# A paged latent-attention decode stage whose cache pages are turned by VectorE in 32 by 32 blocks

## The reference, cut to what matters

```python
c_past = cache_ckv[page_table].reshape(b_s, past_len, KV_RANK)     # 8 x 2048 x 256
kpe_past = cache_kpe[page_table].reshape(b_s, past_len, HEAD_ROPE) # 8 x 2048 x 32
s = einsum('bqhr,bkr->bhqk', q_lat, c) + einsum('bqhe,bke->bhqk', q_pe, kpe)
p = softmax(s * scale)            # 16 heads, 2048 cached positions and the new one
term = einsum('bhqk,bkr->bqhr', p, c)
```

## Time and profile before

| | us |
|---|---|
| median of 3 runs | 2010.53 |
| lowest and highest run | 2008.69, 2016.31 |
| span of the profiled execution | 2007.1 |
| head pairs end, decode loop begins | about 1507 |
| last values of the decode loop end | 1585.1 |

### The profile page before, as it was taken

The page is one execution under the profiler, slowest core; times in us unless marked ns, Lnnn a source line. Parts: engine busy times, 40 slices in busy tenths (PEclk is TensorE's granted clock), DMA queues, the critical chain, the costliest instruction groups (busy, mean ns, idle before and its releaser), DMA issues.

```text
span 2007.1 us, 41612 instructions
## 1 busy us (share of the span) xinstructions
PE 1960.4 (98%) x17604; PEld 1875.2 (93%) x17604; DVE 1277.0 (64%) x1771; ACT 820.4 (41%) x1243; POOL 132.8 (7%) x231
## 2 busy tenths in 40 slices
PE   8999999988999999999999999999989999999999
PEld 7999999987999999999999999997666799999998
DVE  6445486697469577576884856655764349668474
ACT  5332233343245244255452534454654244345252
POOL 3002002010000000000000000000047000000000
PEclk9999999989999999999999999999999999999999
DMA  7233234864342322234322322231248422323222
GB/s 151 84 102 88 75 93 115 269 140 100 95 137 85 120 89 95 77 105 116 97 85 85 127 85 86 84 101 51 54 119 231 149 71 83 127 85 120 91 74 75
DMA packets 260624, 211.55 MB, mean 105 GB/s; under 512 B 42372, under 2 KB 235426, under 8 KB 260450
## 3 DMA queue, kind: packets, MB, share of 16 engines
q1 hardware_dynamic: 248528, 187.52, 31.9%
q0 software_dynamic: 6656, 13.69, 2.4%
q10 hardware_dynamic: 5266, 7.85, 1.2%
HBM read 195.29 MB, written 10.33 MB: 102 GB/s over the span
## 4 chain that ended last, share of the span: by engine, by line
PE 67%; DVE 3%; ACT 2%; issue 2%; SPq 1%; DMA 1%; DVEq 0%; ACTq 0%
PE ps L2459 25%; PE ps L2487 25%; PE ps L2388 6%; PE ps L2401 2%; PE ps L2947 1%; PE ps L3053 1%; PE ps L3209 1%; PE ps L3086 1%; SPq L654 1%; SPq L639 1%; DMA cb<-cache_ckv 1%; PE ps L2841 1%; PE ps L3030 1%; DVE wl L1668 0%; DVE xl L1619 0%
## 5 line engine op out<-in xcount | busy, mean ns | idle before, releaser
L2388 PE MATMUL ps<-xh,wh 128*128 128x260 f32 x1088 | 286.9, 285 | 2.6 <-DVE xl L1619 1.4
L2388 PE MATMUL ps<-xl,wh 128*128 128x260 f32 x1088 | 283.7, 283 | 0.0
L2487 PE MATMUL ps<-xoh,wh 128*128 128x260 f32 x992 | 281.3, 284 | 1.3 <-DVE sq L1835 1.3
L2487 PE MATMUL ps<-xoh,wl 128*128 128x260 f32 x992 | 281.0, 283 | 0.0
L2487 PE MATMUL ps<-xol,wh 128*128 128x260 f32 x992 | 280.6, 283 | 0.0
L2459 PE MATMUL ps<-xh,wh 128*128 128x260 f32 x872 | 228.8, 284 | 0.6 <-DVE wl L1668 0.6
L1067 ACT ACTIVATE wh<-rw 128x1024 fp32r<-128x1024 f32 (+1 forms) x135 | 138.8, 1029 | 218.6 <-PE ps L2459 151.7
L2459 PE MATMUL ps<-xl,wh 128*128 128x260 f32 x872 | 227.0, 282 | 0.0
L2388 PE MATMUL ps<-xh,wl 128*128 128x260 f32 x1088 | 219.3, 283 | 0.0
L990 ACT ACTIVATE wh<-raw 128x1024 fp32r<-128x1024 f32 (+1 forms) x90 | 100.4, 1116 | 283.4 <-PE ps L2388 250.5
L2388 PEld LDWEIGHTS ps<-xh,wh 128*128 128x128 f32 x1088 | 205.6, 189 | 6.9 <-issue 3.9
(11 more groups left out here) (550 smaller groups left out, 4202.2 us busy)
## 6 DMA issues: line engine op xcount, KB each, us to landing
rw<-ffn_w_gate SPq DMA_DIRECT2D x33, 1024.0 KB, 5.4
rw<-ffn_w_up SPq DMA_DIRECT2D x33, 1024.0 KB, 8.0
rw<-ffn_w_down SPq DMA_DIRECT2D x12, 2048.0 KB, 7.8
raw<-ffn_w_gate SPq DMA_DIRECT2D x22, 512.0 KB, 3.9
raw<-ffn_w_up SPq DMA_DIRECT2D x22, 512.0 KB, 3.9
raw<-ffn_w_down SPq DMA_DIRECT2D x16, 704.0 KB, 4.8
rw<-ffn_w_down SPq DMA_DIRECT2D x6, 1536.0 KB, 6.7
cb<-cache_ckv SPq DMA_DIRECT2D x72, 128.0 KB, 3.7
```

The source lines that it names most:

```text
L2388: got = mm(ps[0:width, bank + half, 0:HALF], w[par_][:, k * width:k * width + width], src[:, k0 + k, half * HALF:half * HALF + HALF], star ...
L2487: got = mm(ps[:, bank + mat, T0], w[:, cols], src[:, j, k, :], start=first and k == 0 and m == 0 and s == 0, stop=k == 3 and m == 1, skip_ ...
```

## The change

- A page is read as 32 rows of 4 KB (four tokens each) into 32 partitions: page g goes to the partitions 32 (g mod 4) and up. The rotary key is read as 32 rows of 512 bytes. The number of DMAs and the queue of each stay.
- VectorE turns a sequence in five instructions (`V.transpose`, 32 x 32 blocks): one of 512 elements a partition for the rotary key, four of 1024 for the latent. PSUM, TensorE and ScalarE have no part in it. The 36 TensorE turnings and the 9 copies of a sequence are gone.
- A 32 x 32 block leaves 32 channels on each group of 32 partitions, so the scores become tiles of 32 rows and 32 columns, four row groups by four column groups, 128 tokens in each: 16 matmuls for the rotary key and 32 for each of four parts of the latent, 144 in all (288 records). They write four PSUM banks (0 to 3), one for each row group. There is one set of banks: `past_scores(b, 0)` waits for the exponentials of b - 1.
- The queries are needed on each row group. POOL writes `qlat` to DRAM and reads it back with eight DMAs (`dr_q`, `qrep`), once, before its pages. `qpe` loses its zero padding.
- TensorE's order in one turn is: turning of the probabilities of b, scores of b + 1, values of b. The copy to `pbT` goes from VectorE to ScalarE.
- `wo_half(0, 0, ...)` is split and goes into the last pair of heads and into the first scores. `wide_hi` and `wide_lo` move behind the last probabilities. The banks of `wo_half` and of small tiles change.

```diff
                 for g in ckv:
-                    eng.dma_start(cb[j][:, g, :], inp["cache_ckv"][bass.ds(numbers[b][g], 1)].rearrange("a p r -> p (a r)")).then_inc(arrived[j], 16)
+                    eng.dma_start(page(cb[j], g), inp["cache_ckv"][bass.ds(numbers[b][g], 1)].rearrange(
+                        "a (u v) r -> (a u) (v r)", v=ROWS)).then_inc(arrived[j], 16)
...
+            def turned(b, c):
+
+                if c == 0:
+                    dve.wait_ge(d_in[b % 3], (b // 3 + 1) * 16 * N_SP)
+                    dve.wait_ge(d_kin[b % 3], (b // 3 + 1) * 16 * N_POOL)
                 if b >= 1:
-                    dve.wait_ge(d_s, b)
+                    dve.wait_ge(d_s, (NCT + 1) * (b - 1) + c + 1)
+                if c == 0:
+                    V.transpose(kbT, kb[b % 3].rearrange("p g e -> p (g e)")).then_inc(d_t, 1)
+                else:
+                    V.transpose(cbT[:, c - 1, :, :].rearrange("p q (g u) -> p g q u", u=HP),
+                                cb[b % 3][:, :, 2 * HP * (c - 1):2 * HP * c].rearrange("p g (q r) -> p g q r", q=2)).then_inc(d_t, 1)
...
             for b in range(NB):
-                dve.wait_ge(d_s, b + 1)
-                own(V.tensor_reduce(mb[:, b:b + 1], ps[:, 2 + b % 2, :], AX.X, ALU.max))
+                if b + 1 < NB:
+                    turned(b + 1, 0)
+                    turned(b + 1, 1)
+                dve.wait_ge(d_s, (NCT + 1) * (b + 1))
+                own(V.tensor_reduce(mb[:, b:b + 1], ps[:, 0:NQ, 0:P], AX.XY, ALU.max))
                 ts(nmb[:, b:b + 1], mb[:, b:b + 1], -SCALE, None, ALU.mult).then_inc(d_m, 1)
                 if b + 1 < NB:
-                    turned(b + 1, 1)
-                    turned(b + 1, 3)
-                else:
-                    wide_lo(0)
-                dve.wait_ge(d_pt2, b + 1)
-                if b >= 1:
-                    dve.wait_ge(d_o, b)
-                copy(pbT[:, :, :], ps[:, 4, :].rearrange("p (m q) -> p m q", m=NQ)).then_inc(d_pe, 1)
-                if b + 1 < NB:
-                    turned(b + 1, 5)
-                    turned(b + 1, 7)
+                    for c in range(2, NCT + 1):
+                        turned(b + 1, c)
...
+            def past_scores(b, c):
+
+                if b == 0 and c == 0:
+                    pe.wait_ge(d_qr, 16 * (1 + 2 * NQ))
+                if b >= 1 and c == 0:
+                    pe.wait_ge(d_e, b)
+                pe.wait_ge(d_t, (NCT + 1) * b + c + 1)
+                for q in range(2 if c else 1):
+                    n = 2 * (c - 1) + q
+                    for a in range(NQ):
+                        rows = slice(HP * a, HP * a + HP)
+                        w, keys_ = (qrep[n // NQ][rows, n % NQ, b, :], cbT[rows, c - 1, q, :]) if c else (qpe[rows, b, :], kbT[rows, :])
+                        for j in range(NQ):
+                            got = mm(ps[HP * j:HP * j + HP, a, 0:P], w, keys_[:, P * j:P * j + P],
+                                     start=c == 0, stop=c == NCT and q == 1, skip_group_check=True)
+                got.then_inc(d_s, 1)
```

More of the change, by code:

```diff
@@ L1531, in _ @@
                     act.wait_ge(d_pt2, b)
[L1532 to L1537, removed]
+                run(pb.rearrange("p (v a u) -> p a v u", v=ROWS, a=NQ), ps[:, 0:NQ, 0:P].rearrange("p a (v u) -> p a v u", v=ROWS),
+                    ACT.Exp, bias=nmb[:, b:b + 1], scale=SCALE, accum_out=lb[:, b:b + 1]).then_inc(d_e, 1)
+                if b >= 1:
+                    latents(b - 1)
+                act.wait_ge(d_pt2, b + 1)
+                run(pbT[:, :, :], ps[:, 4, :].rearrange("p (m q) -> p m q", m=NQ), ACT.Copy).then_inc(d_pe, 1)
+            wide_hi(0)
             act.wait_ge(d_w, 1)
@@ L2263, in _ @@
                     maximum(i + 1, 2)
+                else:
+                    turned(0, 0)
                 probs(i, 3)
@@ L3150, in _, with wo_half @@
                     values(1, n // 2)
[L3151 to L3166, removed]
+            def wo_half(d, half, k0, k1):
+                if d == 3 and half == 1:
+                    pe.wait_ge(x_upd, UPD["wo"] + 1)
+                pe.wait_ge(w_lo, WO0 + d + 1)
+                hi_, lo_ = (wh[(WO0 + d) % 2], wl[(WO0 + d) % 2]) if d < 2 else (w4h[:, d - 2], w4l[:, d - 2])
+                for k in range(k0, k1):
+                    for m, (w, srcs_) in enumerate(((hi_, (xh, xl)), (lo_, (xh,)))):
+                        for s, src in enumerate(srcs_):
+                            got = mm(ps[:, WO_BANKS[d][half], 0:HALF], w[:, k * P:k * P + P], src[:, k, half * HALF:half * HALF + HALF],
+                                     start=k == 0 and m == 0 and s == 0, stop=k == KD - 1 and m == 1)
+                if half == 1:
+                    got.then_inc(w_used, 1)
             for i in range(NH // 2):
@@ L3186, in _ @@
                 if not more:
-                    turned(0, 0)
+                    pe.wait_ge(a_ol, NH // 2 - 2)
+                    wo_half(0, 0, 0, 3)
                 turned_probs(i, 4)
+                turned_probs(i, 5)
                 if not more:
-                    turned(0, 1)
-                turned_probs(i, 5)
+                    wo_half(0, 0, 3, NH // 2 - 2)
                 if 2 <= i < NH // 2 - 2:
                     values(i // 2 + 1, i % 2)
-            for q in range(2, 6):
-                turned(0, q)
@@ L3196, in _ @@
             weighted(NH // 2 - 1)
[L3197 to L3210, removed]
-                if half == 1:
-                    got.then_inc(w_used, 1)
@@ L3237, in _ @@
+            for c in range(3):
+                past_scores(0, c)
+            pe.wait_ge(a_ol, NH // 2)
+            wo_half(0, 0, NH // 2 - 2, KD)
+            for c in range(3, NCT + 1):
+                past_scores(0, c)
+            for b in range(NB):
                 pe.wait_ge(d_e, b + 1)
@@ L3243, in _ @@
                 if b + 1 < NB:
-                    for q in range(4, 9):
-                        turned(b + 1, q)
-                else:
-                    turn(ps[0:NB, 7, 0:P], mb[:, :])
-                    turn(ps[0:NB, 7, P:2 * P], lb[:, :]).then_inc(d_rt, 1)
-                    wo_half(1, 0, 0, 3)
+                    for c in range(NCT + 1):
+                        past_scores(b + 1, c)
+                else:
+                    turn(ps[0:NB, 0, 0:P], mb[:, :])
+                    turn(ps[0:NB, 0, P:2 * P], lb[:, :]).then_inc(d_rt, 1)
+                    wo_half(1, 0, 0, 4)
                 pe.wait_ge(d_pe, b + 1)
@@ L3465, in _ @@
                 number(b)
+            pool.wait_ge(l_qe, 1)
+            pool.dma_start(dr_q, qlat[:, :, :, :].rearrange("p r b h -> p r (b h)")).then_inc(d_qr, 16)
+            pool.wait_ge(d_qr, 16)
+            for a in range(NQ):
+                for r in range(RT):
+                    pool.dma_start(qrep[r][HP * a:HP * a + HP].rearrange("p s b h -> p s (b h)"),
+                                   dr_q.rearrange("(s p) r n -> r p s n", s=NQ)[r]).then_inc(d_qr, 16)
             caches()
```

115 lines of the change are left out of this document (45 added, 70 removed).

## The result

The changed kernel takes 2052.12 us (median of 4 runs, 2046.46 to 2055.44), the kernel before 2009.61 beside it: a ratio of 1.0206, with a 95% interval of 1.0187 to 1.0225. It is 42 us slower; 2001.9 was forecast, 50 us less. Its profiled execution took 2046.46 us with a span of 2044.7.

The account below looks back on a forecast made before the run. SyncE's page queue (9.76 us a sequence) was taken as the loop's bound, DMA engines and TensorE close behind. -10.3 + 1.7 = -8.6 us takes 2007.1 to 1998.5; plus 3.4 over the span, 2001.9 us, range 1990 to 2018.

Parts of the forecast that it names:

- Queues: SyncE's page queue: same 17 DMAs, 333 ns an issue, held-up issues go, so a period of 8.76 us.
- a sign of being wrong: Forecast is wrong if VectorE never waits in the loop, SyncE waits long for values, or an issue isn't 333 ns.
- Landing: Time from last page issue to data arrived: taken at 3.7 us with longer rows, bounds 2.5 and 5.8.
- The rival: Page loads into 32 partitions land slower, 200 GB/s instead of 292 at full share: 2017 us, chance 0.07.
- Turning on VectorE: Page transposes on VectorE: 1.22 us per 1024 elements, 5.6 us a sequence; with maximum and negative 6.7 a period.
- Scores: TensorE's 288 small score records take 2.0 to 4.3 us a sequence; only the last part, 0.45 to 0.95, on the path.
- One set of score banks: Scores of b + 1 wait for exponentials of b, about 1.9 us, covered by values of the sequence before (1.9).
- The loop that the buffers close: `pages(b + 3)` waits for values of b: 17.7 us for two periods, 8.8 each, level with the queue; 9.0 taken.
- The clock: TensorE, half idle, may fall to half clock: period taken as 9.0 us instead of 8.8, and 1.7 at the end.
- The start and the end: First maximum at 1510.9, `pages(3)` near 1518.1, `pages(7)` at 1554.1, last probabilities turned at 1571.2 against 1581.48: 10.3 us earlier.

Follow-up runs that it names:

- the last experiment: Changed kernel with old short page rows, maximum ahead of the turnings, and 256-column score tiles (144 records): 2012.01 us, ratio 1.0007 to the kernel before.

## Why the prediction was wrong

**Queues: the price right, the step beside the point.** An issue took 316 ns in the median and nine mostly 4.3 to 4.7 us, as forecast; but held-up issues did not go (up to 1.41 us for one, and 5.48 and 6.36 for nine). And SyncE no longer sets the period: both page queues wait for values, which the forecast had named as a sign of being wrong.

**Landing: taken at 3.7 us, measured 8.4, 6.7 and 5.9 behind the last three issues on the chain.** The rival had the mechanism and the rate: 200 GB/s guessed, 202 measured where the engines were full. Its price was 15 us above the forecast, at a chance of 0.07; alone in the kernel before the rows cost 7 to 9, in the changed kernel 12.5. The Trainium skill, "SBUF — State Buffer", section "Door 1: The DMA port swizzle", gives 189 GB/s for 32 partitions, measured at transfers of 1 MiB. The runs are near it and a little above, with four groups of partitions in flight; I had argued that those would lift it to 292, and they don't.

**Turning on VectorE: right.** 32 transposes of 1024 elements:

```profile
L2256 DVE STREAM_TRANSPOSE cbT<-cb x32: 1201/1203/1236, 1499.7 to 1604.9; 128x1024 f32<-128x1024 f32 x32
```

**Scores: the term that failed most. The record was right, its delivery and its clock were put at nothing.** Between gaps, at a granted clock of 1.00, the starts are 13 ns apart: the group below has 66 starts in 1.16 us less one record's 0.29.

```profile
1526.98 1.16 PE L3215 MATMUL ps<-cbT,qrep 32*32 32x128 f32 x66
```

So the floor of about 25 ns of the Trainium skill ("TensorE: Matmul & The Clock Gate", section "Wait — 56ns, not 53.3ns?") does not hold for matmuls in different tiles, as the earlier trace rows had said. At half clock they are 22 ns apart (128 in 2.80 us above). But the 288 records took 6.6 to 12.6 us a sequence and not 2.0 to 4.3: 2.0 to 5.8 of it idle time for instructions in the sequences on the chain, and the rest at half clock in large part. Neither was in the term for the scores, and instructions were in no rival. The runs put the price of the many small records at 22.2 us, the largest of all. The hint was in the size of the change: 36 turnings and 48 score records became 288 of 13 ns each, so a packet of instructions is used up in 1.7 to 2.8 us.

**One set of score banks: the step that put the scores on the path.** I wrote that the values of the sequence before cover maximum, negative and exponentials, and that only the last part of the scores is on the loop. In TensorE's order those values stand behind the scores of b + 1, and in VectorE's order two turnings of b + 1 stand ahead of the maximum of b. So the exponentials of b, all scores of b + 1 and then the values follow the landing of b + 1, one after another. By the forecast's own prices this mistake was small: two turnings 1.9, maximum to exponentials 1.9, probabilities 0.5 and all scores 2.0 to 4.3 are 6.3 to 8.6 us, where it had 7.2. It became dear by the scores. The maximum ahead of the turnings gave back 9.2 us; the values ahead of the scores gave back nothing.

**The loop that the buffers close: forecast 17.7 us, measured 32.7.** I had put five turnings, the maximum and the last part of the scores on it (7.2 us). In their place stand 15.1: two turnings 1.9, maximum to exponentials 1.6, probabilities 1.1, all scores 10.5 (4.29 of it idle). The landing added 4.7 to its 3.7, the values 3.0 to their 1.9, most of it clock. The sum of the terms was right in form (period = half of this loop) and wrong in three of its entries: the scores by 6 to 8 us, the landing by 4.7, the values by 3.0.

**The clock.** The forecast let its fall cost 0.2 us a period (9.0 for 8.8) and 1.7 us at the end. It is at half for much of the loop (0.70 in the mean of 1507 to 1600): turning and values cost 2.5 us a sequence more. What it would have cost with a period of 9 us isn't shown; with 10.4, in the last experiment, it was at full in four of the seven stretches of 10 us from 1510 to 1580 and the values took 1.86 to 1.91.

**The start and the end.** The first maximum came at 1510.20 against a forecast of 1510.9. `pages(3)` came at 1524.0 and not 1518.1, because the values of sequence 0 already stood behind the scores of 1, 7.8 us with 2.03 idle. From `pages(7)` to the mark it was 29.1 us and not 17.1, by the same terms as in the loop.

What the pieces gave, in us: short rows 12.5, maximum first 9.2, half as many records 22.2, all together 40.1 of 42.5. They overlap, since the short rows also took 12 us off the waits for instructions. How much of the rows' 12.5 is landing and how much is fetch stays open: in the two profiles the landings on the chain are 4.9 us less and the gaps inside the scores on it 7.7 us less (9.5 for 17.2), and some 5 us of that go back to longer issues and the rest of the chain. So does whether a second set of score banks would have paid: it wasn't tried, since a set takes four of the eight banks and the rest hold probabilities, outputs and `wo_half`.

## What to carry to other kernels

Before replacing a few long matmuls by many short ones, count instructions: here TensorE got 256 in some 6 to 8 us beside busy DMA engines (1.9 to 2.8 running, the rest waiting) and in 3.5 to 4.0 us beside quiet ones, whatever its tiles could do. When a change takes a second set of buffers away, write the new order of every engine down for two iterations and look for the first instruction of b + 1 that stands ahead of the last of b; a wait for a transfer in front of it puts the landing into every period. And take DMA rows together with the partitions that they reach: four times longer rows into a quarter of the partitions moved pages a third slower here.

## What the runs showed of the hardware

- TensorE's instructions come in packets of 16 KB, 256 of them, over the same DMA engines as data. In dense code of small matmuls a packet costs a gap, unless TensorE waits for something else meanwhile: 0.6 to 1.8 us with quiet engines, mostly 2.4 to 5.2 beside pages or weights.
- Page loads of 32 partitions by 4 KB ran at about 200 GB/s at full share, 128 partitions by 1 KB at 292.
- Small matmuls in sixteen tiles start 13 ns apart at a granted clock of 1.00 and 22 ns apart at 0.50; in eight tiles (half of the scores) 28 ns apart, 64 starts from 1540.7 to 1542.5, at a granted clock of 0.50.
- `V.transpose` of 128 x 1024 float32 took 1.20 us in 32 x 32 blocks.
- Eight filling records of 3.6 to 5.9 us in all brought the clock back for the work behind them; four of 1.9 to 3.7 us did so too, for the values at 1.93 us.
